# Attention units of a two-block transformer kernel: the output's high part from ScalarE and its low part from VectorE, both read from PSUM

## The chip, the cores and the metric

One NeuronCore of a Trainium2 chip runs the whole kernel as one program. The metric is the device time of one execution in microseconds (us); the median of several executions is given, and one more execution was profiled.

## What is computed

Two transformer blocks over 512 tokens of width 1024. The first has a token mixer (differential attention beside a state-space scan) and a mixture of experts, the second dilated and forgetting attention with convolutional feed-forward layers. The change lies in the differential attention of the first block:

```python
def diff_attend(q, k, v, lam, g_subln, lam_init):
    s = jnp.einsum('bqhcd,bkhcd->bchqk', q.astype(jnp.float32), k.astype(jnp.float32)) * ATTN_SCALE
    p = jax.nn.softmax(s, axis=-1)
    w = p[:, 0] - lam * p[:, 1]
    o = jnp.einsum('bhqk,bkhd->bqhd', w, v.astype(jnp.float32))
    o = o * lax.rsqrt(jnp.mean(o * o, axis=-1, keepdims=True) + EPS) * g_subln.astype(jnp.float32)
    return (o * (1.0 - lam_init)).astype(v.dtype)
```

There are 8 heads, 512 queries and 768 keys (256 of context, 512 of the sequence). Large products are made in float32 precision from two rounded parts: a high part (the value rounded to the type fp32r) and a low part (the value minus its high part, rounded as well).

## The kernel before

`diff_units` runs twice, once for each half of the heads. Each call has U = 16 units, a unit being one tile of 128 queries and one head. In the trace the two calls fill about 472 to 560 us and 652 to 740 us. Each engine has an instruction order of its own, written as a loop over steps i that works on several units at once, and engines wait for each other by semaphores whose values count units.

In step i the engines do this:

- TensorE: the first half of the scores of unit i (L2754, six matmuls, into PSUM banks 0 to 5), the six transposes of the mixed probabilities of unit j = i - 3 (L2777, into banks 6 and 7), the second half of the scores, then the transpose of a finished output (`turn_out`, L2761, into the last quarter of bank 7) and the product with the values (L2801, bank 7). From step 16 on no scores are left, and in steps 16 to 18 matmuls of the next stage (L308, L312, L313) stand in their place; steps 19 to 21 hold only `turn_out`.
- ScalarE: copies of the transposed probabilities (L2820, L2822), the exponentials of unit i - 1 (L2828, two of 128x768), the scaled output of unit j (L2836), then for the output of unit i - 6 `take_out` (L2808: from PSUM times the gain, in float32 to `o_low`), the squares of unit j (L2841), and `high_out` (L2812: `o_low` rounded to `o_high`).
- VectorE: the scaling of an output by its root (L2854), the maxima of unit i - 1 (L2859, 128x1536 from PSUM), a reciprocal and a ratio (L2864, L2865), and the mix of the two probabilities (L2866, 128x768 in SBUF).
- GpSimd: the two parts of the queries of a unit (L2730, L2732), the root of the mean square (L2711, L2713), and `low` (L2717: `o_low` minus `o_high`, the low part).

The tiles have other names in the trace where memory is shared: `oT_low` is `o_low`, `oT_r` is `o_high`, `oT_low_r` is the low part's tile `o_low_r`; `gate_rows` holds outputs and transposed probabilities, `x_tok_r` the parts of queries and keys, `banks` is PSUM. A transpose is recorded as a matmul with `ident`.

The transposes of step i use bank 7, so TensorE waits before them until the output that lay there, that of unit i - 7, has been read (`pe.wait_ge(out_full, j - 3)`, L2775). In the trace that is ScalarE's L2808 in step i - 1. At the end of two steps (`i == U - 4` on ScalarE, `i == U - 3` on VectorE) one weight tile of the next stage is split ahead of time, by L255 on ScalarE and L266 on VectorE (128x2048 each). The call ends with a barrier of all engines.

Of the kernel before, what the change touches and what calls it, by code (L numbers as in the profile page):

```python
# [6 lines left out]
F32 = mybir.dt.float32  # L7
ACT = mybir.ActivationFunctionType
ALU = mybir.AluOpType
AX = mybir.AxisListType.X  # L10

P = 128
# [2645 lines left out]
def diff_units(c, hh, qT, qp, kh, kl, v, o_low, o_parts, ss, lam, gcol, scratch, following, opened):  # L2658
# [6 lines left out]
    with ExitStack() as s:  # L2665
# [18 lines left out]
        squared = c.sem("du_squared")  # L2684
        boxed = c.sem("du_boxed")
        lifted, rooted, scaled = c.sem("du_lifted"), c.sem("du_rooted"), c.sem("du_scaled")
        out_turned, out_full, out_high = c.sem("du_out_turned"), c.sem("du_out_full"), c.sem("du_out_high")
        out_low = c.sem("du_out_low")
        block = s.enter_context(nc.Block())

        def place(to, j):
            tile, h = units[j]
            return to[:, 4 * hh + h, tile * P:(tile + 1) * P]
# [11 lines left out]
        @block.gpsimd  # L2705
        def _(pool):
            def root(j):
                at = slice(j, j + 1)
                pool.wait_ge(parted, 2 * min(j + 6, U))
                pool.wait_ge(squared, j + 1)  # L2710
                nc.gpsimd.tensor_scalar(ss[:, at], ss[:, at], EPS, None, ALU.add).then_inc(lifted, 1)  # L2711
                pool.wait_ge(lifted, j + 1)
                nc.gpsimd.tensor_tensor(ss[:, at], ss[:, at], c.half[:, 0:1], ALU.pow).then_inc(rooted, 1)  # L2713

            def low(j):
                pool.wait_ge(out_high, j + 1)
                nc.gpsimd.tensor_tensor(place(o_low_r, j), place(o_low, j), place(o_high, j).bitcast(F32), ALU.subtract).then_inc(out_low, 1)  # L2717

            def parts(i):
                tile, h = units[i]  # L2720
                if i >= 4:
                    pool.wait_ge(scored, i - 3)
                if i >= 6:
                    pool.wait_ge(rooted, i - 5)
                if i >= 9:
                    pool.wait_ge(out_low, i - 8)
                tok = slice(tile * P, (tile + 1) * P)
                if i:
                    pool.wait_ge(parted, 2 * i)
                nc.gpsimd.tensor_copy(qp[:, i % 4, 0], qT[:, h, tok]).then_inc(parted, 1)  # L2730
                pool.wait_ge(parted, 2 * i + 1)
                nc.gpsimd.tensor_tensor(qp[:, i % 4, 1], qT[:, h, tok], qp[:, i % 4, 0].bitcast(F32), ALU.subtract).then_inc(parted, 1)  # L2732

            for i in range(U + 8):
                if i < U:
                    parts(i)
                if 0 <= i - 5 < U:
                    root(i - 5)
                if i >= 8:
                    low(i - 8)  # L2740

        @block.tensor
        def _(pe):
            def scores_of(i, part):
                h = units[i][1]
                near, far = ((0, 0, 512), (0, 512, ALL)), ((1, 0, 256), (1, 256, ALL))
                order = [(near[0], 0), (far[0], 0), (far[0], 1), (near[0], 1), (far[0], 2), (far[1], 0),
                         (near[0], 2), (far[1], 1), (near[1], 0), (near[1], 1), (far[1], 2), (near[1], 2)]
                for (m, a, z), n in order[6 * part:6 * part + 6]:
                    r = halves_of[m]  # L2750
                    if (m, a, n) == (0, 512, 0):
                        pe.wait_ge(closed, i + 1)
                    q, k = ((0, kh), (0, kl), (1, kh))[n]
                    last = nc.tensor.matmul(scores(i)[:, m * ALL + a:m * ALL + z], qp[r, i % 4, q], k[r, h, a:z], start=n == 0, stop=n == 2)  # L2754
                    if (m, a, n) == (1, 0, 2):
                        last.then_inc(closed, 1)
                return last

            def turn_out(m):
                pe.wait_ge(scaled, m + 1)  # L2760
                nc.tensor.transpose(c.ps[:, 7, 3 * P:4 * P], ob[:, m % 3], c.ident[:]).then_inc(out_turned, 1)  # L2761

            for i in range(U + 6):
                j = i - 3
                if i < U:
                    pe.wait_ge(parted, 2 * i + 2)
                    if i >= 2:
                        pe.wait_ge(expd, 2 * (i - 1))
                    scores_of(i, 0)
                if 0 <= j < U:  # L2770
                    pe.wait_ge(mixed, j + 1)
                    if j:
                        pe.wait_ge(boxed, j)
                    if j >= 4:
                        pe.wait_ge(out_full, j - 3)  # L2775
                    for b in (4, 5, 0, 1, 2, 3):
                        last = nc.tensor.transpose(c.ps[:, 6 + b // 4, (b % 4) * P:(b % 4 + 1) * P], pr[:, j % 3, 0, b * P:(b + 1) * P], c.ident[:])  # L2777
                        if b == 5:
                            last.then_inc(turned_end, 1)
                    last.then_inc(turned, 1)  # L2780
                if i < U:
                    scores_of(i, 1).then_inc(scored, 1)
                elif i in OPENS:
                    if i == U:
                        pe.wait_ge(expd, 2 * (U - 1))
                        opened.take(c, pe)
                    for v2, k in OPENS[i]:
                        opened.step(c, v2, k)
                if j >= U:
                    pe.wait_ge(boxed, U)  # L2790
                    pe.wait_ge(out_full, j - 3)
                    turn_out(j - 3)
                elif j >= 0:
                    h = units[j][1]
                    pe.wait_ge(copied_end, j + 1)
                    if j >= 3:
                        turn_out(j - 3)
                    for b in (4, 5, 0, 1, 2, 3):
                        if b == 0:
                            pe.wait_ge(copied, j + 1)  # L2800
                        last = nc.tensor.matmul(c.ps[:, 7, 2 * P:3 * P], prT[:, j % 2, b], v[:, b, h * P:(h + 1) * P], start=b == 4, stop=b == 3)  # L2801
                    last.then_inc(summed, 1)

        @block.scalar
        def _(act):
            def take_out(m):
                act.wait_ge(out_turned, m + 1)
                nc.scalar.activation(place(o_low, m), c.ps[:, 7, 3 * P:4 * P], ACT.Copy, scale=gcol[:]).then_inc(out_full, 1)  # L2808

            def high_out(m):  # L2810
                act.wait_ge(out_full, m + 1)
                nc.scalar.activation(place(o_high, m), place(o_low, m), ACT.Copy).then_inc(out_high, 1)  # L2812

            for i in range(1, U + 6):
                j, e = i - 3, i - 1
# [19 lines left out]
                        act.wait_ge(out_turned, j - 2)  # L2835
                    nc.scalar.activation(ob[:, j % 3], c.ps[:, 7, 2 * P:3 * P], ACT.Copy, scale=rl[:, j % 4, 0:1]).then_inc(boxed, 1)  # L2836
                if j >= 3:
                    take_out(j - 3)
                if 0 <= j < U:
                    act.wait_ge(boxed, j + 1)  # L2840
                    nc.scalar.activation(sq, ob[:, j % 3], ACT.Square, scale=P ** -0.5, accum_out=ss[:, j:j + 1]).then_inc(squared, 1)  # L2841
                if j >= 3:
                    high_out(j - 3)
                if i == U - 4:
                    c.split.high_ahead(c, act)

        @block.vector
        def _(dve):
            L = lambda ins: c.vlink(dve, ins)
            for i in range(1, U + 5):  # L2850
                e, k, m = i - 1, i - 2, i - 5
                if m >= 0:
                    dve.wait_ge(rooted, m + 1)
                    nc.vector.tensor_scalar(ob[:, m % 3], ob[:, m % 3], ss[:, m:m + 1], None, ALU.mult).then_inc(scaled, 1)  # L2854
                if e < U:
                    dve.wait_ge(scored, e + 1)
                    if e >= 2:
                        dve.wait_ge(expd, 2 * (e - 1))
                    nc.vector.tensor_reduce(mx[:, e % 2], scores(e).rearrange("p (m n) -> p m n", n=ALL), AX, ALU.max, negate=True).then_inc(maxed, 1)  # L2859
                if 0 <= k < U:  # L2860
                    dve.wait_ge(expd, 2 * k + 2)
                    if k >= 4:
                        dve.wait_ge(squared, k - 3)
                    L(nc.vector.reciprocal(rl[:, k % 4], ls[:, k % 3]))  # L2864
                    L(nc.vector.scalar_tensor_tensor(ratio[:, k % 2:k % 2 + 1], rl[:, k % 4, 1:2], lam[:], ls[:, k % 3, 0:1], ALU.mult, ALU.mult))  # L2865
                    nc.vector.scalar_tensor_tensor(pr[:, k % 3, 0], pr[:, k % 3, 1], ratio[:, k % 2:k % 2 + 1], pr[:, k % 3, 0], ALU.mult, ALU.add).then_inc(mixed, 1)  # L2866
                if i == U - 3:
                    c.split.low_ahead(c, dve)

# [1210 lines left out]
```

## Time and profile before

| | |
|---|---|
| median of 3 runs | 3063.06 us (3061.89 to 3063.12) |
| profiled execution, its own time | 3062.65 us |
| span of the profiled execution | 3061.0 us |
| TensorE, VectorE, ScalarE, GpSimd busy | 95%, 58%, 47%, 17% of the span |
| the two calls of the units | 472 to 560 us and 652 to 740 us |

A row of the timeline has start, duration, engine, line, operation and tiles; in brackets stands how long the engine was idle before it and who ended that. Two rows of one engine may overlap by about 0.1 us, since an engine starts an instruction before the one ahead has fully ended.

### The profile page before, as it was taken

Reading aid. Unit: us, or ns where it says so; the run is one execution under the profiler, and the core shown is the slowest. Engines: PE = TensorE matmul, PEld = TensorE weight load, DVE = VectorE, ACT = ScalarE, POOL = GpSimd, SP = SyncE. Lnnn points to the kernel's source line nnn. Section 1 sums busy time; section 2 is a strip of 40 time slices with the busy share of each in tenths; the row PEclk is TensorE's granted clock in tenths of the full one; section 3 lists DMA queues with packets and bytes.
Section 4 is the critical chain, followed back from the end, with each engine's and each line's share of the span. In section 5 each row is a group of like instructions: output and inputs, shape, how many; then the busy total and the mean of one; then the engine's idle time right before and its main releaser. Section 6 shows DMA issues by size and latency. Waiting matters only on the chain. (4 is left out here: it accounts for less than half of the span.)

```text
span 3061.0 us, 38462 instructions
## 1 busy us (share of the span) xinstructions
PE 2918.3 (95%) x15438; PEld 2362.6 (77%) x15438; DVE 1772.6 (58%) x1996; ACT 1435.6 (47%) x1913; POOL 526.8 (17%) x626
## 2 busy tenths in 40 slices
PE   8999999998999899999999899999999998899998
PEld 4878887786887578777777378788888896688887
DVE  4438846445545788888888364555544316455543
ACT  3345627346223478888787133533333325433332
POOL 0006514123101632222222100000000002000000
PEclk9999999999999999999999999999999999999999
DMA  5221011023753589999999551233332301233331
GB/s 208 56 64 42 15 36 56 28 56 97 220 179 110 202 326 372 363 365 373 375 386 354 225 194 42 56 98 97 104 103 69 114 24 47 76 98 95 91 103 42
DMA packets 278385, 456.07 MB, mean 149 GB/s; under 512 B 24864, under 2 KB 206752, under 8 KB 258112
## 3 DMA queue, kind: packets, MB, share of 16 engines
q1 hardware_dynamic: 251712, 398.82, 37.8%
q0 software_dynamic: 26496, 54.79, 4.9%
q8 instruction: 123, 2.02, 0.3%
q14 instruction: 54, 0.44, 0.0%
HBM read 451.16 MB, written 39.08 MB: 160 GB/s over the span
## 5 line engine op out<-in xcount | busy, mean ns | idle before, releaser
L266 DVE TENSOR_TENSOR weight_part<-weights,weight_part 128x2048 fp32r<-128x2048 f32 (+1 forms) x61 | 138.3, 2267 | 157.4 <-ACT weight_part L255 157.4
L1188 ACT ACTIVATE up_conv<-banks,tap_columns 128x512 f32<-128x512 f32 x88 | 68.5, 778 | 292.4 <-PE banks L313 292.4
L255 ACT ACTIVATE weight_part<-weights 128x2048 fp32r<-128x2048 f32 (+1 forms) x61 | 114.1, 1870 | 169.6 <-PE banks L308 164.1
L776 POOL TENSOR_SCALAR branch_mean<-branch_mean 128x1 f32<-128x1 f32 x20 | 10.4, 521 | 1057.2 <-ACT up_conv L770 713.3
L1232 DVE SCALAR_TENSOR_TENSOR up_conv<-banks,tap_columns,up_conv 128x511 f32<-128x511 f32 x88 | 66.0, 750 | 218.0 <-ACT up_conv L1188 218.0
L308 PE MATMUL banks<-hT_r,weight_part 128*128 128x512 f32 x432 | 171.1, 396 | 1.8 <-DVE weight_part L266 1.4
L313 PE MATMUL banks<-hT_r,weight_part 128*128 128x512 f32 x432 | 169.9, 393 | 0.0
L266 DVE TENSOR_TENSOR weight_part_o<-weights,weight_part_o 128x2048 fp32r<-128x2048 f32 (+2 forms) x46 | 100.0, 2175 | 117.8 <-ACT weight_part_o L255 117.8
L308 PE MATMUL banks<-hT_r,weight_part_o 128*128 128x512 f32 x384 | 151.0, 393 | 0.0
L313 PE MATMUL banks<-hT_r,weight_part_o 128*128 128x512 f32 x384 | 150.2, 391 | 0.0
L312 PE MATMUL banks<-h_low,weight_part_o 128*128 128x512 f32 x384 | 149.1, 388 | 0.0
L312 PE MATMUL banks<-h_low,weight_part 128*128 128x512 f32 x384 | 149.1, 388 | 0.0
L3326 POOL DMA_INDIRECT gathered<-h_tokens,block_rows x64 | 104.2, 1628 | 211.7 <-PE banks L3443 196.6
L3438 PE MATMUL banks<-weights_r,gatheredT_r 128*128 128x512 f32 x336 | 132.0, 393 | 0.0
L255 ACT ACTIVATE weight_part_o<-weights 128x2048 fp32r<-128x2048 f32 (+2 forms) x46 | 83.7, 1820 | 97.8 <-PE banks L308 88.8
L3331 POOL DMA_INDIRECT expert_rows<-lent,block_rows x64 | 65.8, 1028 | 230.7 <-ACT lent L3681 222.7
L3437 PE MATMUL banks<-gate_up_high,gatheredT_r 128*128 128x512 f32 x256 | 103.6, 405 | 0.0
L3437 PE MATMUL banks<-h_tokens_r,gatheredT_r 128*128 128x512 f32 x256 | 103.6, 405 | 0.0
L3713 DVE TENSOR_TENSOR weights_r<-weights,h_tokens_r 128x2048 fp32r<-128x2048 f32 x42 | 95.4, 2290 | 13.9 <-ACT h_tokens_r L3610 12.5
L3713 DVE TENSOR_TENSOR weights_r<-weights,gate_up_high 128x2048 fp32r<-128x2048 f32 x42 | 95.3, 2290 | 12.8 <-ACT gate_up_high L3610 12.5
L3439 PE MATMUL banks<-gate_up_high,lent_r 128*128 128x512 f32 x256 | 101.4, 396 | 0.0
L3439 PE MATMUL banks<-h_tokens_r,lent_r 128*128 128x512 f32 x256 | 101.4, 396 | 0.0
(742 smaller groups left out, 8874.9 us busy)
## 6 DMA issues: line engine op xcount, KB each, us to landing
weights<-in_w_e_gate SPq DMA_DIRECT2D x44, 1024.0 KB, 15.3
weights<-in_w_e_up SPq DMA_DIRECT2D x44, 1024.0 KB, 13.6
hT<-in_w_e_down SPq DMA_DIRECT2D x44, 1024.0 KB, 11.9
weights<-in_w_up SPq DMA_DIRECT2D x88, 512.0 KB, 5.1
gate_up<-in_w_e_gate SPq DMA_DIRECT2D x22, 1024.0 KB
gate_up<-in_w_e_up SPq DMA_DIRECT2D x22, 1024.0 KB
down<-in_w_e_down SPq DMA_DIRECT2D x22, 1024.0 KB
weights<-in_w_down SPq DMA_DIRECT2D x20, 1024.0 KB, 5.0
```

What stands on the lines that cost most here:

```text
L255: c.nc.scalar.activation(self.pair(n)[0][:, 0:z], self.raw[n % RAW_SLOTS][:, 0:z], ACT.Copy).then_inc(self.high_ready, 1)
L266: c.nc.vector.tensor_tensor(low[:, 0:z], self.raw[n % RAW_SLOTS][:, 0:z], high[:, 0:z].bitcast(F32), ALU.subtract).then_inc(self.low_ready, 1)
L308: ins = c.nc.tensor.matmul(out, lhs[0], rhs[0], start=start, stop=False)
L312: c.nc.tensor.matmul(out, lhs[0], rhs[1], start=False, stop=False)
L313: return c.nc.tensor.matmul(out, lhs[1], rhs[0], start=False, stop=stop)
L1188: nc.scalar.activation(a[:, f % 2, v], c.ps[:, 2 * (f % 4) + v], ACT.Identity, scale=conv[:, 2, ch:ch + 1], bias=bias[:, ch:ch + 1]).then_ ...
L1232: nc.vector.scalar_tensor_tensor(a[:, f % 2, v, 1:], c.ps[:, 2 * (f % 4) + v, 0:SEQ - 1], conv[:, 1, ch:ch + 1], a[:, f % 2, v, 1:], ALU.m ...
L3326: nc.gpsimd.indirect_dma_start(xg[n % 2][:], None, h_dram, bass.IndirectOffsetOnAxis(tab[:, n, 0:1], 0), bounds_check=SEQ - 1, oob_is_err= ...
L3437: nc.tensor.matmul(out, lhs[0], rhs[0], start=start, stop=False)
L3438: nc.tensor.matmul(out, lhs[0], rhs[1], start=False, stop=False)
L3439: return nc.tensor.matmul(out, lhs[1], rhs[0], start=False, stop=stop)
L3713: nc.vector.tensor_tensor(gu_low[i][:, v], gu[i][:, v], gu_high[n % 2][:, v].bitcast(F32), ALU.subtract).then_inc(gu_parted, 1)
```

## The change

The float32 copy of an output in `o_low` is gone. `high_out` now reads PSUM itself and writes the rounded high part. The low part is made on VectorE by `low_out`, one instruction that reads PSUM again, multiplies by the gain and subtracts the high part. GpSimd has no part in it any more. Since VectorE is now the last reader of the output in bank 7, TensorE waits for `out_low` in place of `out_full`.

```diff
@@ GpSimd
-            def low(j):
-                pool.wait_ge(out_high, j + 1)
-                nc.gpsimd.tensor_tensor(place(o_low_r, j), place(o_low, j), place(o_high, j).bitcast(F32), ALU.subtract).then_inc(out_low, 1)
...
-                if i >= 9:
-                    pool.wait_ge(out_low, i - 8)
...
-            for i in range(U + 8):
+            for i in range(U + 5):
...
-                if i >= 8:
-                    low(i - 8)
@@ TensorE
-                        pe.wait_ge(out_full, j - 3)
+                        pe.wait_ge(out_low, j - 3)
...
-                    pe.wait_ge(out_full, j - 3)
+                    pe.wait_ge(out_low, j - 3)
@@ ScalarE
-            def take_out(m):
+            def high_out(m):
                 act.wait_ge(out_turned, m + 1)
-                nc.scalar.activation(place(o_low, m), c.ps[:, 7, 3 * P:4 * P], ACT.Copy, scale=gcol[:]).then_inc(out_full, 1)
-
-            def high_out(m):
-                act.wait_ge(out_full, m + 1)
-                nc.scalar.activation(place(o_high, m), place(o_low, m), ACT.Copy).then_inc(out_high, 1)
+                nc.scalar.activation(place(o_high, m), c.ps[:, 7, 3 * P:4 * P], ACT.Copy, scale=gcol[:]).then_inc(out_high, 1)
@@ VectorE
+            def low_out(m):
+                dve.wait_ge(out_high, m + 1)
+                nc.vector.scalar_tensor_tensor(place(o_low_r, m), c.ps[:, 7, 3 * P:4 * P], gcol[:], place(o_high, m).bitcast(F32), ALU.mult, ALU.subtract).then_inc(out_low, 1)
...
+                    if i >= 7:
+                        low_out(i - 7)
                     nc.vector.scalar_tensor_tensor(pr[:, k % 3, 0], pr[:, k % 3, 1], ratio[:, k % 2:k % 2 + 1], pr[:, k % 3, 0], ALU.mult, ALU.add).then_inc(mixed, 1)
+                elif i >= 7:
+                    low_out(i - 7)
```

Where the new instruction stands on VectorE is seen in the order of one step in the middle of a call. Before, from the scaling of an output to the next one:

```order
L2854 TENSOR_SCALAR gate_rows<-gate_rows,sum_squares 128x128 [waits du_rooted_179]
L2859 TENSOR_REDUCE minus_maxima<-banks 128x2 [waits du_exp_169,du_scored_166]
L2864 RECIPROCAL one_over_sums<-sums 128x2 [waits du_squared_176,du_exp_169]
L2865 SCALAR_TENSOR_TENSOR ratios<-one_over_sums,minus_lambda,sums 128x1 [waits vector_step_4]
L2866 SCALAR_TENSOR_TENSOR probs<-probs,ratios 128x768 [waits vector_step_4]
```

The same step on VectorE now, from step 7 on:

```order
L2844 TENSOR_SCALAR gate_rows<-gate_rows,sum_squares 128x128 [waits du_rooted_179]
L2849 TENSOR_REDUCE minus_maxima<-banks 128x2 [waits du_exp_169,du_scored_166]
L2854 RECIPROCAL one_over_sums<-sums 128x2 [waits du_squared_176,du_exp_169]
L2855 SCALAR_TENSOR_TENSOR ratios<-one_over_sums,minus_lambda,sums 128x1 [waits vector_step_4]
L2838 SCALAR_TENSOR_TENSOR oT_low_r_3610<-banks,subln_gain,oT_r_3609 128x128 [waits du_out_high_182,vector_step_4]
L2858 SCALAR_TENSOR_TENSOR probs<-probs,ratios 128x768
```

The low part has come in behind the maxima, the reciprocal and the ratio, and ahead of the mix, with a wait for ScalarE's high part.

On ScalarE the piece from the scaled output to the next copy of transposed probabilities read before:

```order
L2836 ACTIVATE gate_rows<-banks,one_over_sums 128x128 [waits du_out_turned_181,du_squared_176,du_summed_175]
L2808 ACTIVATE oT_low<-banks,subln_gain 128x128 [waits du_out_turned_181]
L2841 ACTIVATE gate_rows,sum_squares<-gate_rows 128x128 [waits du_boxed_177]
L2812 ACTIVATE oT_r_3609<-oT_low 128x128 [waits du_out_full_182]
L2820 ACTIVATE gate_rows<-banks 128x256 [waits du_summed_175,du_turned_last_tiles_172]
```

And now, at the same place:

```order
L2824 ACTIVATE gate_rows<-banks,one_over_sums 128x128 [waits du_out_turned_181,du_squared_176,du_summed_175]
L2800 ACTIVATE oT_r_3609<-banks,subln_gain 128x128 [waits du_out_turned_181]
L2829 ACTIVATE gate_rows,sum_squares<-gate_rows 128x128 [waits du_boxed_177]
L2808 ACTIVATE gate_rows<-banks 128x256 [waits du_summed_175,du_turned_last_tiles_172]
```

The read from PSUM keeps its place and now makes the high part; the second instruction behind the squares is gone.

## Rows read from the trace of the kernel before

**Rows 1.** The page, section 1: busy time of each engine over the span

```profile
PE 2918.3 (95%) x15438; PEld 2362.6 (77%) x15438; DVE 1772.6 (58%) x1996; ACT 1435.6 (47%) x1913; POOL 526.8 (17%) x626
```

**Rows 2.** L2777's idle time in both calls: released by, us in total, times

```profile
  ACT oT_low L2808: 4.8, 6
```

**Rows 3.** Timeline of a unit in steady state: steps 10 and 11, first call

```profile
507.14 1.02 DVE L2866 SCALAR_TENSOR_TENSOR probs<-probs,ratios 128x768 f32<-128x768 f32 x1
...
507.35 0.88 PE L2777 MATMUL banks<-ident,probs 128*128 128x128 f32 x6
507.52 0.71 POOL L2711 TENSOR_SCALAR sum_squares<-sum_squares 128x1 f32<-128x1 f32 x1 [1.45 <-ACT gate_rows L2841]
507.83 0.38 ACT L2820 ACTIVATE gate_rows<-banks 128x256 f32<-128x256 f32 x1 [0.26 <-PE banks L2777]
...
508.86 0.46 POOL L2717 TENSOR_TENSOR oT_low_r<-oT_low,oT_r 128x128 fp32r<-128x128 f32 x1
508.92 0.47 DVE L2854 TENSOR_SCALAR gate_rows<-gate_rows,sum_squares 128x128 f32<-128x128 f32 x1 [0.77 <-POOL sum_squares L2713]
...
509.32 1.74 DVE L2859 TENSOR_REDUCE minus_maxima<-banks 128x2 f32<-128x1536 f32 x1
...
510.77 0.47 PE L2754 MATMUL banks<-x_tok_r 64*128 64x512 f32 x2 [0.17 <-ACT probs L2828]
510.91 0.36 ACT L2808 ACTIVATE oT_low<-banks,subln_gain 128x128 f32<-128x128 f32 x1
...
511.43 1.02 DVE L2866 SCALAR_TENSOR_TENSOR probs<-probs,ratios 128x768 f32<-128x768 f32 x1
...
511.56 0.88 PE L2777 MATMUL banks<-ident,probs 128*128 128x128 f32 x6
```

**Rows 4.** Timeline of VectorE in step 5, before GpSimd makes low parts

```profile
488.03 0.29 DVE L2854 TENSOR_SCALAR gate_rows<-gate_rows,sum_squares 128x128 f32<-128x128 f32 x1 [0.76 <-POOL sum_squares L2713]
...
488.23 1.75 DVE L2859 TENSOR_REDUCE minus_maxima<-banks 128x2 f32<-128x1536 f32 x1
```

**Rows 5.** Timeline of the weight tile that is split ahead, steps 13 and 14

```profile
524.06 0.31 ACT L2812 ACTIVATE oT_r<-oT_low 128x128 fp32r<-128x128 f32 x1
...
524.15 0.87 PE L2777 MATMUL banks<-ident,probs 128*128 128x128 f32 x6
524.26 1.91 ACT L255 ACTIVATE oT_r<-weights 128x2048 fp32r<-128x2048 f32 x1
...
526.20 2.29 DVE L266 TENSOR_TENSOR oT_low_r<-weights,oT_r 128x2048 fp32r<-128x2048 f32 x1 [0.88 <-ACT oT_r L255]
...
528.64 1.74 DVE L2859 TENSOR_REDUCE minus_maxima<-banks 128x2 f32<-128x1536 f32 x1
...
529.62 0.87 PE L2777 MATMUL banks<-ident,probs 128*128 128x128 f32 x6
```

**Rows 6.** Timeline of the end of the first call and the next stage's start

```profile
558.18 0.47 DVE L2854 TENSOR_SCALAR gate_rows<-gate_rows,sum_squares 128x128 f32<-128x128 f32 x1 [5.43 <-POOL sum_squares L2713]
...
558.80 0.30 PE L2761 MATMUL banks<-ident,gate_rows 128*128 128x128 f32 x1 [0.76 <-DVE gate_rows L2854]
559.14 0.37 ACT L2808 ACTIVATE oT_low<-banks,subln_gain 128x128 f32<-128x128 f32 x1 [0.35 <-PE banks L2761]
...
559.92 0.45 POOL L2717 TENSOR_TENSOR oT_low_r<-oT_low,oT_r 128x128 fp32r<-128x128 f32 x1 [0.53 <-ACT oT_r L2812]
560.73 0.77 PE L308 MATMUL banks<-hT_r,oT_r 128*128 128x512 f32 x1 [1.63 <-PEq L2665]
```

**Rows 7.** Groups of VectorE with 128x128 from PSUM: busy us, mean ns

```profile
L2426 DVE TENSOR_TENSOR masked_CB<-banks,triangles 128x128 f32<-128x128 f32 x16 | 4.7, 291 | 14.8 <-PE banks L2361 14.8
...
L383 DVE TENSOR_SCALAR yT<-banks,ssd_gain 128x128 f32<-128x128 f32 x16 | 4.4, 345 | 2.9 <-PE banks L395 2.9
```

**Rows 8.** Windows: busy us of PE, PEld, DVE, ACT, POOL, granted clock, DMA

```profile
478.00:482.00 4.00, 4.00 (x22) 3.45 (x23) 2.97 (x4) 1.61 (x5) 0.00 (x0) 0.50 1.08 354
499.00:524.10 25.10, 24.12 (x187) 19.63 (x186) 20.12 (x30) 23.04 (x67) 14.67 (x30) 1.00 0.00 1
```

More of the change, by code:

```diff
@@ L2686, in diff_units @@
         lifted, rooted, scaled = c.sem("du_lifted"), c.sem("du_rooted"), c.sem("du_scaled")
-        out_turned, out_full, out_high = c.sem("du_out_turned"), c.sem("du_out_full"), c.sem("du_out_high")
+        out_turned, out_high = c.sem("du_out_turned"), c.sem("du_out_high")
         out_low = c.sem("du_out_low")
@@ L2837, in _ @@
                 if j >= 3:
-                    take_out(j - 3)
+                    high_out(j - 3)
                 if 0 <= j < U:
@@ L2841, in _ @@
                     nc.scalar.activation(sq, ob[:, j % 3], ACT.Square, scale=P ** -0.5, accum_out=ss[:, j:j + 1]).then_inc(squared, 1)
-                if j >= 3:
-                    high_out(j - 3)
                 if i == U - 4:
@@ L2849, in _ @@
             L = lambda ins: c.vlink(dve, ins)
-            for i in range(1, U + 5):
+            def low_out(m):
+                dve.wait_ge(out_high, m + 1)
+                nc.vector.scalar_tensor_tensor(place(o_low_r, m), c.ps[:, 7, 3 * P:4 * P], gcol[:], place(o_high, m).bitcast(F32), ALU.mult, ALU.subtract).then_inc(out_low, 1)
+            for i in range(1, U + 7):
                 e, k, m = i - 1, i - 2, i - 5
-                if m >= 0:
+                if 0 <= m < U:
                     dve.wait_ge(rooted, m + 1)
```

## The prediction

> **What bounds the kernel now.** The page's busy times come first: TensorE is busy in 95% of the span [rows 1], so a gap on TensorE is the only thing that this change can make or close. Next I read the line of the transposes, L2777. It shows six waits for ScalarE's L2808, 4.8 us in all, 0.8 each [rows 2]: steps 16 to 18 of either call, where no scores stand ahead of the transposes. Both calls run the same program, so I work out one and double it.
>
> Then the timeline of a unit in steady state [rows 3]. Call T the start of the transposes of a step. From T = 507.35 to the next T = 511.56 is 4.20 us (to 0.01), and the loop that takes them is this: transposes, ScalarE's copies (from 507.83) and exponentials, then 0.17 us of waiting until TensorE may overwrite the scores (510.77), six score matmuls (0.79 us), next T. ScalarE idles 0.26 us ahead of L2820 in each turn, so it is not full: it does its small instructions (L2836, L2808, L2841, L2812) while TensorE makes scores. L2808 runs 510.91 to 511.27. A wait of TensorE costs 0.15 us from the end of what it waits for: L2854 ends at 558.65, and the transpose behind it starts at 558.80 [rows 6]. So `out_full` is good at 511.42, just 0.14 us ahead of T. That is all the cover there is.
>
> VectorE has a loop of its own beside it: mix at 507.14 and at 511.43, 4.29 us apart [rows 3]. In it GpSimd's L2711 ends only at 508.23, 0.07 us behind the end of the mix (508.16); then come L2713, for which VectorE waits 0.77 us, L2854 at 508.92, the maxima 0.40 us after that, and the mix 2.11 us after the maxima. So VectorE is nearly full too.
>
> **The change part by part.**
>
> *Removed on ScalarE: L2812.* About 0.3 us a unit, in front of an idle stretch of 0.26 us [rows 3]: worth nothing by itself. ScalarE would wait for TensorE a bit longer. Only where L255 follows does it let something start earlier, by 0.20 us (L2812 began at 524.06, L255 behind it at 524.26) [rows 5]; that is in the sum below.
>
> *Removed on GpSimd: L2717, 0.46 us.* GpSimd sits idle 1.45 us a unit [rows 3], so its own time is free. But L2854, started 0.06 us behind L2717, took 0.47 us and let the maxima start 0.40 us later; where no L2717 stood there, it took 0.29 us and the maxima came after 0.20 us [rows 4]. VectorE's loop becomes 0.20 us shorter.
>
> *The high part.* Same place, same source, same shape as L2808, so 0.36 us: no change.
>
> *Added on VectorE: the low part.* No row of this kind with 128x128 exists. The nearest are a tensor-tensor from PSUM of that size, 291 ns, and a tensor-scalar from PSUM with a per-partition factor, 345 ns [rows 7]. The new one has both the factor and the second tensor; I take 0.34, with 0.28 and 0.47 (the held L2854) as the ends.
>
> The Trainium skill gives a formula for it ("VectorE: DVE Perf Modes", section on the TRN2 errata): 120 cycles plus the elements for a PSUM source at 0.96 GHz, an estimate of 258 ns. Both rows of this size are longer; by the page's figure the time would be 30 x 0.08 = 2.4 us lower than my sum.
>
> *The moved wait.* The transposes now wait for the low part, behind L2808's successor and behind VectorE's queue. It can start at the later of (a) the high part's end plus 0.03 us (as L266 starts 0.03 us behind the end of L255 [rows 5]), 511.30, and (b) the mix's old place, 2.11 us behind the maxima. With the maxima 0.20 us earlier, (b) is 511.23, so (a) decides. It ends at 511.64, and T comes 0.15 us later: 511.79 in place of 511.56. That is **0.24 us** a unit, a period of 4.44. VectorE's own loop is then 4.29 - 0.20 + 0.26 (the new instruction less the overlap) = 4.35 us and still fits. It counts in steps 7 to 13 and 15, since the first low part is in step 7: 8 x 0.24 = 1.92 us.
>
> *Step 14, behind the split weight tile.* Before, T went from 524.15 to 529.62 because ScalarE had L255 in its way; VectorE's L266 (526.20) pushed the maxima to 528.64, but TensorE did not need VectorE there [rows 5]. Now it does. L255 starts 0.20 earlier, so the maxima start at 528.44, the low part at 530.55, it ends at 530.89, T = 531.04. That is 1.42 us later than 529.62, of which 0.24 is the shift of step 13 counted already: **1.18 us**.
>
> *Steps 16 to 18.* T stood right behind L2808 (the three waits a call of [rows 2]); now the low part lies between: 0.03 + 0.34 = 0.37 each, **1.11 us**.
>
> *The end of a call.* Three last outputs go through one corner of bank 7 in turn. Before: L2854 at 558.18, transpose 558.80, L2808 559.14, GpSimd's last low part ends 560.37, 2.19 us from L2854's start, and 0.36 us later the next stage begins [rows 6]. Now L2854 (0.28) is followed on VectorE by low part 13 (0.34), and only then may output 14 be transposed; each further output costs 0.15 + 0.34 + 0.37 + 0.03 + 0.34 = 1.23 us. That is 0.28 + 0.34 + 2 x 1.23 = 3.08 less 0.05 overlap: 3.03, **0.84 us** more. It is on the path, as all engines meet there and TensorE was idle for 1.63 us.
>
> Sum of a call: 1.92 + 1.18 + 1.11 + 0.84 = 5.05 us; both calls 10.1 us. Against the profiled execution's own time that is 3062.65 + 10.1 = 3072.75. That execution lies 0.41 us below the median of 3063.06, so the number to compare is **3073.2 us**, 0.33% slower.
>
> **The rivals.**
>
> *A. Faster: ScalarE is the bound, and each L2812 removed shortens the loop.* That would give 16 x 0.3 x 2 = 9.6 us, about 3053.5. It decides only if ScalarE had no idle time ahead of L2820; the row shows 0.26 us [rows 3]. The wait that moved would also have to be free. Chance 0.05.
>
> *B. The low part lands in time, or nearly.* Then only the ends of the calls cost, 1.7 us: 3064.8. From 511.30 to 511.41 there are 0.11 us for an instruction whose nearest rows take 0.29. For it speaks only that a handoff between VectorE and TensorE in mid-stream may be shorter than 0.15, or that step 14 finds VectorE less late. Somewhere between this and my sum, up to 3069, I put 0.17.
>
> *C. VectorE's loop becomes the bound.* If L2854 is still held by GpSimd (now by L2730, the next in its queue), the loop is 4.29 + 0.26 = 4.55 us in place of 4.44: 8 x 0.11 x 2 = 1.8 us more; with the long price of the low part (0.47), 3.9 more. That is 3075 to 3079. Chance 0.13.
>
> The Trainium skill says of the port pair that VectorE and GpSimd share ("SBUF — State Buffer", section on the two separate sides) that whoever starts first holds it for its whole instruction. The rows of L2711 and L2854 [rows 3, 4] agree. By that rule L2730, which must first wait for L2713's own semaphore, comes behind L2854 and is held itself, as I assume.
>
> *D. TensorE's clock falls.* At 478 to 482 us, after a long wait, the granted clock was 0.50; in steady state it is 1.00 [rows 8]. Step 14 now leaves TensorE idle for 1.4 us between scores and transposes. If the clock fell there, a few units would be longer by up to a microsecond each: about 3076. Nothing in the profile shows it after a gap so short in this call. Chance 0.05.
>
> **How the numbers follow.** My forecast has 0.60, A 0.05, B 0.17, C 0.13, D 0.05. The forecast's own range follows from the low part's ends (0.28: 30 x 0.06 = 1.8 us less; 0.47: 3.9 more) and from step 14: 3070 to 3077. For 8 in 10, B's upper part and C are taken in: 3067 to 3078. A measurement of this kernel can tell about 0.2%, 6 us, from no change. Slower than 3069.2: forecast, C, D and none of B, 0.78 less a little for doubt in step 14: 0.77. Within 6 us: B and that rest, 0.17. Faster: 0.06.
>
> **What would show it.** In the profile after: T to T about 4.44 us in steps 7 to 13, with TensorE's idle time ahead of the transposes put down to VectorE's new line, 0.2 to 0.3 us a unit; the new instruction at 0.34 us, 0.03 behind the high part; L2854's successor at 0.28; step 14 at about 6.65 us from T to T; the call's last instruction on VectorE, not GpSimd, and a longer idle stretch ahead of the next stage's first matmul. Wrong it would be if the period stayed at 4.20 (B), if the new instruction started behind the ratio rather than behind the high part (C), or if TensorE's matmuls in steps 14 and 15 took twice their time (D).

## The result, and the profile after

The changed kernel took 3079.91 us in the median (3075.52 to 3082.17, 5 runs), the kernel before 3063.06 us (3061.89 to 3068.37, 5 runs). The ratio is 1.0054 with a 95% interval of 1.0041 to 1.0067. The direction was as forecast. The time lies above the range's upper end of 3078, and the increase of 16.9 us stands against 10.1 forecast. The profiled execution took 3080.45 us.

The page after, section 1, busy time of each engine:

```profile
PE 2916.8 (95%) x15438; PEld 2360.1 (77%) x15438; DVE 1778.3 (58%) x2028; ACT 1429.0 (46%) x1881; POOL 524.8 (17%) x594
```

The counts are the change itself: 32 more instructions on VectorE, 32 fewer on ScalarE and on GpSimd. The sums of busy time say nothing of where 17 us went; the answer to [rows 2] shows 10.3 us of it. It is the line of the transposes, now L2769, with its idle time by releaser in both calls:

```profile
its engine sat idle before it (us, times) until:
...
  DVE oT_low_r L2838: 15.1, 24
```

Before, TensorE waited for the last reader of bank 7 six times, 4.8 us. Now it waits 24 times, 15.1 us, and the one it waits for is VectorE's new instruction.

The timeline of a step in steady state answers to [rows 3] (steps 9 and 10 of the first call; L2858 is the mix, L2844 the scaling, L2849 the maxima, L2800 the high part, L2838 the low part):

```profile
505.23 1.01 DVE L2858 SCALAR_TENSOR_TENSOR probs<-probs,ratios 128x768 f32<-128x768 f32 x1
505.31 1.01 POOL L2711 TENSOR_SCALAR sum_squares<-sum_squares 128x1 f32<-128x1 f32 x1 [1.82 <-ACT gate_rows L2829]
505.46 0.84 PE L2769 MATMUL banks<-ident,probs 128*128 128x128 f32 x6 [0.24 <-DVE oT_low_r L2838]
505.91 0.38 ACT L2808 ACTIVATE gate_rows<-banks 128x256 f32<-128x256 f32 x1 [0.76 <-PE banks L2769]
...
507.01 0.29 DVE L2844 TENSOR_SCALAR gate_rows<-gate_rows,sum_squares 128x128 f32<-128x128 f32 x1 [0.77 <-POOL sum_squares L2713]
...
507.21 1.75 DVE L2849 TENSOR_REDUCE minus_maxima<-banks 128x2 f32<-128x1536 f32 x1
...
508.99 0.36 ACT L2800 ACTIVATE oT_r<-banks,subln_gain 128x128 fp32r<-128x128 f32 x1
...
509.45 0.35 DVE L2838 SCALAR_TENSOR_TENSOR oT_low_r<-banks,subln_gain,oT_r 128x128 fp32r<-128x128 f32 x1 [0.17 <-ACT oT_r L2800]
...
509.95 0.85 PE L2769 MATMUL banks<-ident,probs 128*128 128x128 f32 x6 [0.25 <-DVE oT_low_r L2838]
```

The chain reads from below: TensorE starts 0.15 us behind the low part's end (509.80), the low part starts 0.10 us behind the high part's end (509.35). The wait for the high part is an instruction of its own here. The answer for the line `dve.wait_ge(out_high, m + 1)`:

```profile
L2837 DVEq EVENT_SEMAPHORE  x22: 21/21/21, 495.9 to 730.2; - x22
```

Of the 32 low parts, 22 have this separate wait ahead of them: those of steps 7 to 17, which wait for the ratio as well. In all of them but three (the two of step 14, and step 10 of the second call, see below) the gap behind the high part is 0.10 us. The other ten, in the last steps of a call, carry the wait themselves; in eight of them VectorE is free and the gap is 0.03 us, in two VectorE is still busy with L2844 and it is 0.36. From T to T it is 4.49 us, before 4.20. ScalarE now idles 0.76 us ahead of its first copy where it idled 0.26: the time saved by L2812 and the time lost by TensorE both became idle time on ScalarE. L2844 takes 0.29 us and the maxima come 0.20 us behind it, as without L2717.

Step 14, behind the split weight tile, answers to [rows 5]:

```profile
523.00 1.92 ACT L255 ACTIVATE oT_r<-weights 128x2048 fp32r<-128x2048 f32 x1
...
523.42 0.84 PE L2769 MATMUL banks<-ident,probs 128*128 128x128 f32 x6 [0.25 <-DVE oT_low_r L2838]
...
524.95 2.29 DVE L266 TENSOR_TENSOR oT_low_r<-weights,oT_r 128x2048 fp32r<-128x2048 f32 x1 [0.75 <-ACT oT_r L255]
...
527.39 1.75 DVE L2849 TENSOR_REDUCE minus_maxima<-banks 128x2 f32<-128x1536 f32 x1
...
529.50 0.35 DVE L2838 SCALAR_TENSOR_TENSOR oT_low_r<-banks,subln_gain,oT_r 128x128 fp32r<-128x128 f32 x1
...
530.00 0.30 PE L2769 MATMUL banks<-ident,probs 128*128 128x128 f32 x1 [1.56 <-DVE oT_low_r L2838]
```

The low part has no idle time ahead of it here: it was ready to run and stood behind L266 and the maxima in VectorE's queue. TensorE idled 1.56 us for it. Step 14 came 6.58 us behind step 13 (before 5.47).

The end of the first call answers to [rows 6]:

```profile
560.12 0.29 DVE L2844 TENSOR_SCALAR gate_rows<-gate_rows,sum_squares 128x128 f32<-128x128 f32 x1 [0.97 <-POOL sum_squares L2713]
560.33 0.34 DVE L2838 SCALAR_TENSOR_TENSOR oT_low_r<-banks,subln_gain,oT_r 128x128 fp32r<-128x128 f32 x1
560.77 0.30 PE L2753 MATMUL banks<-ident,gate_rows 128*128 128x128 f32 x1 [1.22 <-DVE oT_low_r L2838]
561.11 0.37 ACT L2800 ACTIVATE oT_r<-banks,subln_gain 128x128 fp32r<-128x128 f32 x1 [1.15 <-PE banks L2753]
...
562.70 0.35 DVE L2838 SCALAR_TENSOR_TENSOR oT_low_r<-banks,subln_gain,oT_r 128x128 fp32r<-128x128 f32 x1 [0.84 <-ACT oT_r L2800]
...
563.37 0.76 PE L308 MATMUL banks<-hT_r,oT_r 128*128 128x512 f32 x1 [1.11 <-PEq L2665]
```

Three engines take turns for each of the last outputs, 1.19 us a turn (560.77 to the next transpose at 561.96). Here TensorE starts 0.10 us behind the low part's end (560.67 to 560.77), not 0.15.

**Where the time came in.** I cut both profiled executions at the same points: T of step 6 in each call, the first matmul of the next stage behind each call, and the first and last VectorE instructions of the mixture of experts (in the kernel before 985 to 1735 us). All in us, by difference of start times; the last row runs to the execution's own time, which is 1.7 us longer than the span:

| stretch | before | after | difference |
|---|---|---|---|
| start to step 6 of call 1 | 494.8 | 492.0 | -2.8 |
| call 1, step 6 to next stage | 65.97 | 71.40 | **+5.4** |
| next stage to step 6 of call 2 | 113.3 | 111.5 | -1.8 |
| call 2, step 6 to next stage | 67.08 | 74.41 | **+7.3** |
| to the mixture of experts | 243.4 | 243.7 | +0.3 |
| mixture of experts | 750.1 | 760.2 | +10.1 |
| rest, to the end | 1328.0 | 1327.3 | -0.7 |

The two calls make 12.8 us. The other 5 us net come from stretches where no instruction was changed, the largest of them 10.1 us in the mixture of experts. The first question for the experiments was therefore whether the change caused these too.

In the second call two steps stand out: from step 9 to 10 it took 4.84 us, and from step 14 to 15 6.02 us where the first call took 4.49. Windows of TensorE in step 14 to 15, first call and second call (busy us of PE, PEld, DVE, ACT, POOL, granted clock, DMA share, GB/s):

```profile
530.00:534.49 4.49, 4.08 (x31) 3.27 (x32) 3.52 (x7) 3.67 (x10) 0.15 (x1) 1.00 0.02 4
...
713.22:719.24 6.02, 5.54 (x32) 4.48 (x32) 3.53 (x7) 3.67 (x10) 0.15 (x1) 0.72 0.01 1
```

The same 31 or 32 matmuls took 5.54 us instead of 4.08, at a mean granted clock of 0.72: for a little over half of the stretch TensorE was at 1.2 GHz instead of 2.4. This is the prediction's rival D, in one of the two calls.

### The profile page after: what moved, and what is told of

Its sections match the earlier page's. It is cut to its first block and busy times, and to the rows that moved or that the text cites. A ratio compares the mean times of both kernels' runs of the same rounds, so it can differ in the third digit from the quotient of the medians.

```text
span 3078.8 us, 38438 instructions
## 1 busy us (share of the span) xinstructions
PE 2916.8 (95%) x15438; PEld 2360.1 (77%) x15438; DVE 1778.3 (58%) x2028; ACT 1429.0 (46%) x1881; POOL 524.8 (17%) x594
## 5 line engine op out<-in xcount | busy, mean ns | idle before, releaser
L266 DVE TENSOR_TENSOR weight_part<-weights,weight_part 128x2048 fp32r<-128x2048 f32 (+1 forms) x61 | 138.4, 2268 | 155.0 <-ACT weight_part L255 154.9
L266 DVE TENSOR_TENSOR weight_part_o<-weights,weight_part_o 128x2048 fp32r<-128x2048 f32 (+2 forms) x46 | 100.1, 2176 | 117.8 <-ACT weight_part_o L255 117.8
L3707 DVE TENSOR_TENSOR weights_r<-weights,gate_up_high 128x2048 fp32r<-128x2048 f32 x42 | 95.1, 2290 | 11.5 <-ACT gate_up_high L3604 11.5
```

The lines of the kernel that those rows point to most:

```text
L266: c.nc.vector.tensor_tensor(low[:, 0:z], self.raw[n % RAW_SLOTS][:, 0:z], high[:, 0:z].bitcast(F32), ALU.subtract).then_inc(self.low_ready, 1)
L3707: nc.vector.tensor_tensor(gu_low[i][:, v], gu[i][:, v], gu_high[n % 2][:, v].bitcast(F32), ALU.subtract).then_inc(gu_parted, 1)
```

## The experiments

### Both kernels once more

No edit. These two runs ask what an execution of the same program varies by.

> The kernel before, unchanged, once more. The profile after showed the two calls of the units 12.8 us longer (step 6 to the next stage's first matmul), but also 2.8 us less ahead of the first call, some 2 us less after it, and about 9 us more in the mixture of experts (1004 to 1766 us), where nothing was changed. Theory N, chance: those other differences vary from execution to execution, so this profile of the same program shows a mixture of experts that differs by several us from the 762 us of the first profile, or runs that spread by 5 us and more. Theory C, caused: the program of before always gives 762 us there within 1 us, and 3062 to 3064 us in all.

> The changed kernel, unchanged, once more. Both theories expect the calls at 5.4 us (first) and 5.4 to 7.3 us (second) above before, with a period of 4.49 us. Theory N expects the stage of the mixture of experts anywhere within 762 to 772 us and a ratio between 1.003 and 1.006. Theory C expects 771 us there again and a ratio of 1.0054.

| stretch (us) | before | c_before | after | c_after |
|---|---|---|---|---|
| start to step 6 | 494.8 | 492.5 | 492.0 | 494.8 |
| call 1 | 65.97 | 65.98 | 71.40 | 71.37 |
| to step 6 of call 2 | 113.3 | 111.5 | 111.5 | 111.4 |
| call 2 | 67.08 | 67.09 | 74.41 | 74.47 |
| mixture of experts | 750.1 | 749.5 | 760.2 | 753.4 |
| rest, to the end | 1328.0 | 1329.8 | 1327.3 | 1333.7 |

The copy of before ran at a median of 3065.54 us, ratio 1.0000 (0.9987 to 1.0012). The kernel before itself, in 34 other runs beside these, had a median of 3066.15 and ran from 3057.06 to 3073.45: the first three runs, within 1.2 us of each other, did not show this spread. The changed kernel came to 3079.02 us, ratio 1.0043 (1.0029 to 1.0058).

Theory N holds in its main point: the mixture of experts took 753.4 us the second time, not 760; over all nine profiles of this study (each with its own variant of the calls) it took 745.8 to 760.2 us, the start 492.0 to 496.6 and the rest 1327.2 to 1337.0. (The 762 us of the expectation counted from 1004 to 1766 us; the cut of the table gives 750.) One half of the expectation did not come: the second profile of before shows 749.5 us there, within 1 us of the first, as theory C had it; but its runs spread over 12 us, which theory C excluded. The calls, in contrast, repeat to 0.1 us, with the slow step 15 and the 4.84 us step of the second call in both profiles. So the effect that the profiles show of the change is the 12.8 us in the calls: 3066.15 + 12.8 = 3079.0, against 3079.02 measured. That they agree so closely is luck; the interval of 1.0029 to 1.0058 allows 9 to 18 us.

A part of the other differences is TensorE's granted clock. The first 12 us of the next stage behind the first call, in before, c_before and after (columns as above):

```profile
560.73:572.73 12.00, 10.58 (x31) 7.93 (x32) 2.89 (x2) 4.90 (x4) 0.00 (x0) 0.65 0.61 175
...
558.49:570.49 12.00, 10.57 (x39) 8.02 (x40) 4.13 (x5) 4.92 (x4) 0.00 (x0) 0.86 0.61 175
...
563.37:575.37 12.00, 10.57 (x39) 8.02 (x40) 4.12 (x5) 4.91 (x4) 0.00 (x0) 0.87 0.62 175
```

Where the mean clock there was 0.86 or 0.87 (four of the nine profiles), the stretch up to step 6 of the second call took 111.4 to 111.5 us; where it was 0.62 to 0.67 (the other five), 112.9 to 113.7. The unchanged kernel shows both, so this 1.8 us is not of the change.

### ScalarE's part alone

```diff
-                nc.scalar.activation(place(o_low, m), c.ps[:, 7, 3 * P:4 * P], ACT.Copy, scale=gcol[:]).then_inc(out_full, 1)
...
-                nc.scalar.activation(place(o_high, m), place(o_low, m), ACT.Copy).then_inc(out_high, 1)
+                nc.scalar.activation(place(o_high, m), c.ps[:, 7, 3 * P:4 * P], ACT.Copy, scale=gcol[:]).then_inc(out_high, 1)
...
-                        pe.wait_ge(out_full, j - 3)
+                        pe.wait_ge(out_high, j - 3)
```

> Only ScalarE's part of the change: the high part is made straight from PSUM and TensorE waits for it as it did for the full copy, while GpSimd still writes a low part, now the high part minus itself, so the low part of every attention output is left out (zero). The theory that ScalarE was not the bound expects the period of a unit to stay at 4.20 us, 0.2 us less at the split weight tile and 0.3 us less at the end of each call, 1 us in all: 3062. The rival that ScalarE bounds the loop expects 0.3 us a unit, 9.6 us: 3053. If code layout of these calls is what lengthens the mixture of experts, its time should move here too, by up to 9 us.

GpSimd's line, not shown above, subtracts the high part from itself, so the kernel leaves out the low part of every output of the units. The number and the size of its instructions stay. The median was 3066.68 us, ratio 1.0001 (0.9987 to 1.0015). The calls took 65.35 and 66.53 us, 1.2 us less than before together; the period stayed at 4.20, step 14 went from 5.46 to 5.26. Two answers, the lines of ScalarE's first copy from 498 to 524 us, before and in this kernel (busy us, mean ns, idle us ahead of it):

```profile
L2820 ACT ACTIVATE gate_rows<-banks 128x256 f32<-128x256 f32 x6 | 2.3, 384 | 1.6 <-PE banks L2777 1.6
```

```profile
L2816 ACT ACTIVATE gate_rows<-banks 128x256 f32<-128x256 f32 x6 | 2.3, 384 | 2.8 <-PE banks L2777 2.8
```

Six turns, 1.2 us more idle time: 0.2 us a turn of what L2812 held went into waiting for TensorE, nothing into the period. Rival A is out. The run also says that the high part made from PSUM, taken alone, costs nothing that can be measured.

### VectorE's work without the moved wait

```diff
+            def low(m):
+                dve.wait_ge(out_high, m + 1)
+                nc.vector.tensor_tensor(place(o_low_r, m), place(o_low, m), place(o_high, m).bitcast(F32), ALU.subtract).then_inc(out_low, 1)
...
                     nc.vector.scalar_tensor_tensor(pr[:, k % 3, 0], pr[:, k % 3, 1], ratio[:, k % 2:k % 2 + 1], pr[:, k % 3, 0], ALU.mult, ALU.add).then_inc(mixed, 1)
+                if i >= 7:
+                    low(i - 7)
```

GpSimd's `low` and its waits are taken out as in the change; ScalarE's and TensorE's code is that of before.

> Only VectorE's extra work, without the moved wait: ScalarE keeps the full copy and the rounded copy, TensorE waits for the full copy as before, and VectorE makes the low part from SBUF behind the mix instead of GpSimd. If the moved wait is the cause, TensorE's period stays at 4.20 us and steps 16 to 18 are as before: 0 to 3 us more in all, from VectorE's longer loop (4.29 - 0.20 + 0.28 = 4.37 us a unit, against a slack of 1.6 us ahead of the exponentials, so that it shows in the last units only if at all). The rival that VectorE's added work is the cause expects most of the 4.49 us period here too, some 5 us a call.

The median was 3062.78 us, ratio 0.9997 (0.9981 to 1.0014). The calls took 65.59 and 66.78 us, 0.7 us less than before. VectorE has 32 more instructions here too, yet every step has its old length (4.20, 5.46, 4.06, 6.60, 6.60). TensorE's waits from 498 to 560 us show why:

```profile
PE banks L2769 <- ACT oT_low L2800: 2.4, 3, 0.8
```

These are the three waits of before, and none for VectorE. The 0.4 us less at each end (9.24 against 9.66 from step 18 to the next stage) has two parts: the last scaling of an output on VectorE takes 0.29 us where it took 0.47, and the last low part is shorter (0.29 us on VectorE, 0.45 on GpSimd). This low part reads SBUF alone; no run has VectorE read PSUM without the moved wait. The transposes themselves are no slower in the changed kernel (six in 0.84 us, before in 0.88), so nothing here shows a cost of that read beside the wait. This version is ahead of both kernels in the calls, by an amount that the whole time can't tell from nothing.

### The low part behind the mix

```diff
-                    if i >= 7:
-                        low_out(i - 7)
                     nc.vector.scalar_tensor_tensor(pr[:, k % 3, 0], pr[:, k % 3, 1], ratio[:, k % 2:k % 2 + 1], pr[:, k % 3, 0], ALU.mult, ALU.add).then_inc(mixed, 1)
-                elif i >= 7:
+                if i >= 7:
                     low_out(i - 7)
```

> The changed kernel with the low part moved behind the mix on VectorE (1.0 us later in its queue), everything else as it is. If the wait of the transposes for the low part sets the period, it grows from 4.49 us to about 5.25 us (low part at 4.8 us behind the last transposes, 0.35 for it, 0.14 to TensorE) in steps 7 to 15: 8 x 0.77 x 2 = 12 us more than the changed kernel, 1.009 to before. The rival that VectorE's total work, not its place in the queue, costs the time expects no change, 1.0043 to 1.0054.

The median was 3093.79 us, ratio 1.0102 (1.0087 to 1.0118). The same instructions, one of them a place later in its queue, took 14 us more than the changed kernel (in the median, of 4 and 5 runs); the calls took 81.73 and 79.47 us. The period was 5.21 us, as expected of a wait that sets it: 8 x 0.72 x 2 = 11.5 us of the difference. One turn of this kernel:

```profile
504.91 1.02 DVE L2856 SCALAR_TENSOR_TENSOR probs<-probs,ratios 128x768 f32<-128x768 f32 x1
505.85 0.35 DVE L2838 SCALAR_TENSOR_TENSOR oT_low_r<-banks,subln_gain,oT_r 128x128 fp32r<-128x128 f32 x1
...
506.34 0.85 PE L2769 MATMUL banks<-ident,probs 128*128 128x128 f32 x6 [0.97 <-DVE oT_low_r L2838]
```

Here the low part does not wait for the high part; it follows the mix, and TensorE idles 0.97 us. The clock fell in this kernel too, but in the first call: step 14 to 15 took 7.04 us and step 16 to 17 8.53, while the second call had 5.21 and 6.95.

### The weight tile behind the low part

```diff
                     if i >= 7:
                         low_out(i - 7)
+                    if i == U - 2:
+                        c.split.low_ahead(c, dve)
                     nc.vector.scalar_tensor_tensor(pr[:, k % 3, 0], pr[:, k % 3, 1], ratio[:, k % 2:k % 2 + 1], pr[:, k % 3, 0], ALU.mult, ALU.add).then_inc(mixed, 1)
...
-                if i == U - 3:
-                    c.split.low_ahead(c, dve)
```

> The changed kernel with VectorE's part of the weight tile that is split ahead (L266, 2.3 us) moved from the end of step 13 to step 14, behind the low part and ahead of the mix. If the 1.1 us that step 14 costs is L266 standing ahead of the low part, step 14's transposes come about 5.25 us behind step 13's, where ScalarE's part leaves them, and not 6.57; but VectorE has no room, so that the next maxima are late and step 15 takes about 6.0 us and not 4.49. Sum of the two 11.2 us, against 11.07 us in the first call of the changed kernel: no gain, 1.004 to 1.0055. The rival that the wait in step 14 comes from ScalarE or TensorE expects step 14 at 6.57 us still. If TensorE's clock falls in the second call for the gap of step 14 alone, it should now fall a step later or not at all.

The median was 3081.68 us, ratio 1.0055 (1.0035 to 1.0074). Step 14 came 5.14 us behind step 13 (6.58 in the changed kernel), step 15 6.26 us behind that, in both calls: 11.40 us together against 11.07. So L266 ahead of the low part is what step 14 waited for, and there is no place for its 2.3 us on VectorE once TensorE waits there in each step. The clock now fell a step later, in the first call (6.04 us from step 15 to 16), not in the second; windows of steps 14 to 15 and 15 to 16, columns as above:

```profile
531.47:537.73 6.26, 4.09 (x32) 3.29 (x32) 5.73 (x8) 3.66 (x10) 4.12 (x4) 1.00 0.01 3
537.73:543.77 6.04, 4.78 (x26) 4.13 (x26) 3.52 (x7) 3.66 (x10) 0.15 (x1) 0.72 0.00 0
...
724.38:728.86 4.48, 3.22 (x25) 2.71 (x26) 3.52 (x7) 3.66 (x10) 0.15 (x1) 1.00 0.02 4
```

The last row is step 15 to 16 of the second call, at full clock.

### A shorter idle stretch in step 14

```diff
                     scores_of(i, 0)
+                    if i == U - 2:
+                        scores_of(i, 1).then_inc(scored, 1)
...
-                    scores_of(i, 1).then_inc(scored, 1)
+                    if i != U - 2:
+                        scores_of(i, 1).then_inc(scored, 1)
```

> The changed kernel, with TensorE making both halves of the scores of unit 14 ahead of the transposes of step 14 instead of one half on either side, so that its idle stretch of 1.5 us there shrinks by 0.85 us. In both profiles of the changed kernel the second call has 6.0 us from step 14 to step 15 with TensorE at twice its usual matmul times, the first call 4.49 us. The theory that the long wait lets TensorE's clock fall expects 4.49 us in both calls, call two at 73.0 us instead of 74.4. The rival that something else in the second call slows these matmuls expects 6.0 us again. The start of step 14's transposes stays where it was (6.57 us behind step 13), as VectorE's low part sets it.

The median was 3080.45 us, ratio 1.0055 (1.0041 to 1.0068). Step 14 came 6.57 us behind step 13, as expected. Step 14 to 15 took 4.36 us in the first call and 5.20 in the second. Neither number of the expectation: not 4.49 and not 6.01. TensorE's row at the start of step 14's transposes in the second call, and the window of that step:

```profile
717.67 1.29 PE L2771 MATMUL banks<-ident,probs 128*128 128x128 f32 x6 [1.02 <-DVE oT_low_r L2841]
...
717.67:722.87 5.20, 4.72 (x26) 4.29 (x26) 3.53 (x7) 3.67 (x10) 0.15 (x1) 0.67 0.02 5
```

The clock fell again, to a mean of 0.67, in the step behind the long wait. It cost 0.84 us against the first call instead of 1.53, since a half of the scores was already made and fewer matmuls (26, not 32) stood in that step. The idle stretch ahead of step 14 was 1.02 us, against 1.55 in the changed kernel: shorter by 0.53 us, not by the 0.85 of the expectation, and that did not keep the clock up. In the first call the same stretch, 1.03 us, was followed by no fall.

## Why the prediction was wrong, step by step

The mechanism was right: a moved wait, exposed because only 0.14 us of cover stood ahead of T. Three steps of the prediction failed. The sum had no term for a fall of TensorE's clock, and it came: 1.53 us. The moved wait was taken as 0.24 us a unit, with a start 0.03 us behind the high part; the start came 0.10 us behind it, and the wait cost 0.29. And the forecast stood on a base of 3063.06 us from three runs, with no term for the spread of the executions, which then ran from 3057 to 3073 us.

The wait is the cause of the time in the calls: without it VectorE's extra work costs nothing (0.9997), ScalarE's part costs nothing (1.0001), and making it later by one instruction adds 14 us. The terms per call, from the profiles after and before:

| term | predicted | call 1 | call 2 |
|---|---|---|---|
| steps 7 to 13 and 15 | 1.92 | 2.33 | 4.22 |
| step 14 | 1.18 | 1.11 | 1.12 |
| steps 16 to 18 | 1.11 | 1.27 | 1.29 |
| end of the call | 0.84 | 0.70 | 0.70 |
| sum | 5.05 | 5.4 | 7.3 |

Over both calls the difference from the forecast's 10.1 us is 2.6: 1.53 for the clock, 0.8 for the moved wait, 0.35 for one step, 0.3 more in steps 16 to 18, and 0.4 less in step 14 and at the ends.

*The moved wait, period 4.44.* It was 4.49. The low part takes 0.351 us in the median, so 0.34 was good; the estimate of 258 ns by the Trainium skill's formula ("VectorE: DVE Perf Modes", section on the TRN2 errata) is 0.09 us short in this trace. What was off is its start, 0.10 us behind the high part's end, not 0.03. The 0.03 was read from L266, which waits for one engine only; in these steps the low part has the separate wait of L2837 ahead of it. Less 0.03 us by which the high part itself ended earlier in a step, that is 0.05 us in each of 16 steps, 0.8 us.

*Rival D, TensorE's clock.* I gave it 0.05, and the sum left it out ("Nothing in the profile shows it after a gap so short"). It happened in the second call, in both profiles of the changed kernel: 1.53 us. This is the largest error inside the calls. The prediction's reason, that no gap so short had been followed by a fall, was a reading of the trace before and not a bound: behind gaps of 1.0 to 2.7 us the clock now fell in one call and stayed up in the other.

*One step that no part of the prediction had.* From step 9 to 10 of the second call, 4.84 us instead of 4.49 in both profiles: the low part started 0.46 us behind the high part instead of 0.10. It costs 0.35 us. The separate wait (L2837) was over at its usual time, 0.40 us before the low part started, where the usual step has 0.04 (wait at 696.76 and low part at 697.18, one step earlier 692.27 and 692.33); so ScalarE was not late. Why VectorE started late is open.

*VectorE's loop, rival C.* It stayed inside: maxima 0.20 us behind L2844, low part waiting 0.17 us for ScalarE. The long form of it did not come. L2711 was held by the mix in each turn (505.31 to 506.32, the mix to 506.24), as counted on.

*The end of a call* cost 0.70 us, not 0.84: a turn took 1.19 us instead of 1.23, since TensorE starts 0.10 us behind the low part there and not 0.15, and the next stage began 0.32 us behind the last low part and not 0.36.

*Rival B's number*, 3064.8, counted the ends of the calls alone. Steps 16 to 18 have no cover at all (0.8 us of waiting each before), so their 1.11 us a call belong to B as well: about 3067.

*ScalarE's saving* was worth nothing in a step, as forecast, and 0.2 us at the split tile (5.46 to 5.26 in e_high).

*The number to compare.* 0.4 us were added for the median of three runs, 3063.06. In 34 other runs the median is 3066.15, 3.1 us higher (3064.53 in nine more, 3064.9 in eight). From there the forecast's 10.1 us give 3076.3, and the 12.8 us of the calls 3079.0. The range of 3067 to 3078 took in the bounds of the costs, but nothing for the spread of the executions, and leaned on "a measurement can tell 0.2%" only for the chances. Neither error alone put the result outside: 3063.06 + 12.8 is 3075.9, and 3066.15 + 10.1 is 3076.3, both within the range. The two together did, and how much of the 16.9 us first measured belongs to the spread (4.1 us by these numbers) is known no better than the intervals allow. The first ratio, 1.0054, has in its baseline those early low runs; the later one, 1.0043, agrees with 12.8 us of 3066 (1.0042), and so does the first within its interval.

## What to carry to other kernels

When a buffer's last reader changes, follow the buffer's next writer: the price is how much later the release comes than the old one, less the cover that the old one had (here the release came 0.42 us later in a step, 4.34 us behind T instead of 3.92, against a cover of 0.14), not the length of the new instruction. One full copy out of PSUM that looks wasteful may be what frees the bank early: with it the low part could be made from SBUF at no cost (0.9997), without it a second reader held the bank. And put the spread of the executions into a range before the costs: three runs within 1.2 us said nothing of it here.

## What the hardware showed that I had not expected

- TensorE's granted clock fell to means of 0.58 to 0.80 over the step behind a long wait (step 14; step 15 where the weight tile stood later; steps 14 and 16 with the low part behind the mix), in every kernel in which TensorE waits for VectorE in each step, and in one of the two calls only; which one depended on the kernel. The idle time ahead of it was 1.02 us (shorter idle stretch), 1.55 (changed kernel), 2.00 (weight tile later), 2.66 and 1.99 (low part behind the mix), and the other call had the same idle times at a clock of 1.00. In the four profiles without that wait (both of before, ScalarE's part alone, VectorE's work alone) all steps kept their length. What decides is open. The kernel with the low part behind the mix, step 14 to 15 of either call:

```profile
539.34:546.38 7.04, 6.69 (x31) 5.52 (x32) 3.47 (x6) 3.66 (x10) 0.08 (x1) 0.58 0.01 2
...
734.47:739.68 5.21, 4.08 (x31) 3.28 (x32) 3.38 (x6) 3.66 (x10) 0.79 (x2) 1.00 0.02 5
```

- An instruction on VectorE that waits for ScalarE and is already at the head of its queue starts 0.03 us behind the other's end where it carries the wait itself (L266 [rows 5], L2838 in the last steps of a call), and 0.10 us behind it where the wait is an instruction of its own (L2837) because it waits for a second thing too.
- Stretches with no change in them vary between executions by up to 14 us (mixture of experts, 745.8 to 760.2 us), while the attention calls repeat to 0.1 us. A comparison by stretch settles here what the whole time leaves within 0.3%.
